# Group norm by chunks of tokens inside the first projection, sample states beside it, and outputs ahead of transposes in the prompt's attention

## The chip, the cores and the metric

The kernel runs on one core of one Trainium2 chip. The time is device microseconds of one execution. TensorE (PE in the rows) multiplies; VectorE (DVE), ScalarE (ACT) and GpSimd (POOL) work on elements; SyncE (SP) issues DMAs. Each engine works through a program of its own, in order, and the programs meet at semaphores.

## The reference, cut to what matters

One inference step of a decoder of two layers, for a prompt of 512 tokens and 8 samples of 4 new tokens: 544 token columns. All is float32; D_MODEL is 1024. Layer 0 mixes a gated convolution with retention in 4 heads:

```python
h, gate_b, gate_c, q, k, v, g = _split(x @ w_in, EVEN_SPLITS)      # 7 x 512 columns
u, conv_hist = causal_dwconv(gate_c * h, conv_hist, conv_w, conv_b)
y_a = gate_b * u
o, ret_state = retention(q, k, v, ret_state, log_gamma)            # chunks of 128 tokens
mu = jnp.mean(o, axis=-1, keepdims=True)                           # over the 128 of a head
var = jnp.mean(jnp.square(o - mu), axis=-1, keepdims=True)
o = ((o - mu) * lax.rsqrt(var + LN_EPS)).reshape(b, t, -1) * gn_g
y_b = jax.nn.silu(g) * o
y = jnp.concatenate([y_a, y_b], axis=-1) @ w_out
```

The samples' matrix state is updated too: 8 samples x 4 heads of 128x128, `state * gamma**4 + k_dec.T @ v`. Layer norms and convolved feed-forward layers follow, and layer 1 has an attention of three branches, whose prompt part is of interest here: softmax over up to 512 keys in a selected and a window branch, then the product with the values.

## The kernel before

Activations lie transposed: features on the 128 partitions, tokens along the row of 544 (`T`), as two halves of 272 (`HT`). A product streams its weights in pieces of 128x1024. ScalarE copies a piece to a rounded high part (`hi`, L1544) and VectorE subtracts to get the low part (`lo`, L1713). TensorE then makes one *stripe* (128 output features): 8 parts of k, each with high x high, high x low and low x high, in two halves, 48 matmuls at L1325, into banks 0 and 1 or 2 and 3 of PSUM. ScalarE takes the even stripes from PSUM into `big` (L1548), VectorE the odd ones (L1720).

The first projection `in0` has 28 stripes: q 0 to 3, k 4 to 7, v 8 to 11, g 12 to 15, c 16 to 19, h 20 to 23, b 24 to 27. After each of the last 16 a *gap* g = 0 to 15 follows, in which TensorE, ScalarE and VectorE run `retention_gap(g)` of their own program. TensorE does the gap's matmuls before the next stripe. The other two do theirs after the `hi` or `lo` of two stripes ahead and after their take, while TensorE is at the next stripe. Gaps 0 to 3 do the rotation, 4 to 11 retention in four chunks of 128 tokens (an even gap: transposes and scores, L1408 to L1418; an odd one: outputs and state, L1430 to L1436), 12 and 13 the same for the samples (13 with 64 small products against the sample states, L1464). Banks 4 to 7 serve these gaps. Gaps 14 and 15 are empty.

GpSimd does the convolution of the four rows c = 0 to 3 (L1993 to L2008). Each waits for stripe 20 + c, multiplies, sums three taps, stores the history, waits for the gate's stripe 24 + c, multiplies by it (L2007, L2008), and only then begins the next row.

After stripe 27 comes the stretch that the change is about, in which no stripe runs. `big[QZ:QZ+4]` are the four heads' outputs over all 544 tokens. Head by head: a mean over partitions as a product with a constant matrix (L1511), subtraction (L1830), square (L1605), a second product (L1519), square root (L1612), reciprocal (L1840), scaling (L1843), the gate (L1847), then the rounded high part on ScalarE (L1599) and the low part on VectorE (L1823). The gate's Silu (L1591) and the convolution's high and low parts (L1594, L1816) come first. Between the heads stand the sample states: VectorE spreads the values (`spread_values`, L1801), TensorE makes two products of 512 columns a head (`state_product`, L1500), VectorE adds them to the states (`new_states`, L1810). TensorE waits for all eight updates, then starts the product `out0`, whose k parts 0 to 3 are the convolution's rows and 4 to 7 the heads. A part can start when its low part is there (`mix_lo`).

In layer 1 the prompt's attention runs 8 rounds of 8 units u (four query tiles, in the order 3,3,0,0,2,2,1,1, each in two branches). A unit is: scores `s` on TensorE (L611), mask and maximum `a` on VectorE (L1036, L1038), exponential `e` on ScalarE (L851), normalization `b` on VectorE (L1046 to L1053), transposes `t` on TensorE (L621), their copy `ta` on ScalarE (L859), outputs `o` on TensorE (L635, L640). TensorE's order in a unit is s(u+2), t(u), o(u-1). VectorE's is b(u), a(u+2); ScalarE's is e(u+1), ta(u). Both t(u) and o(u-1) wait for ta(u-1); t(u) waits for b(u) as well.

## Time and profile before

| | us |
|---|---|
| three runs | 1950.58, 1959.45, 1958.18 |
| median | 1958.18 |
| the profiled execution's own time | 1950.48 |
| its span, first to last instruction | 1948.9 |
| mean granted TensorE clock, share of full | 0.948 |
| stretch from the end of stripe 27 to the first matmul of out0 | 219.52 to 266.06 |

Times of single steps are counted from the start of the span. TensorE is busy for 92% of the span, VectorE for 50%, ScalarE for 35%, GpSimd for 19%. A granted clock of 1.0 is 2.4 GHz and one of 0.5 is 1.2 GHz. The granted clock of a stretch is the mean over it. Matmul ends are modelled, so TensorE's busy time is not all work at its peak.

### The profile page before, as it was taken

What the parts mean: (1) busy time and instruction counts of PE and PEld (TensorE: products, weight loads), DVE (VectorE), ACT (ScalarE), POOL (GpSimd) and SP (SyncE); (2) the same over time, 40 slices, a digit from 0 to 9 for tenths busy, and PEclk for the clock granted to TensorE, in tenths of its full rate; (3) what the DMA queues carried; (4) which work ended last, traced back from release to release, by engine and by line L of the source; (5) the groups of instructions that cost most, each with busy time, mean ns of one, the idle gap of its engine ahead of it and who ended that gap; (6) DMA issues with size and microseconds to landing.
All of it is one profiled execution on the core that took longest, in us unless ns stands there. A gap on an engine that the chain in (4) does not pass through costs nothing.

```text
span 1948.9 us, 34969 instructions
## 1 busy us (share of the span) xinstructions
PE 1793.6 (92%) x13070; PEld 1610.5 (83%) x13070; DVE 980.8 (50%) x1456; ACT 691.2 (35%) x1209; POOL 367.1 (19%) x580
## 2 busy tenths in 40 slices
PE   8999787999999997997888898998979799999996
PEld 8999667999999997996555566665659799999996
DVE  3353287544443435224777755646553644444434
ACT  3222223333332223223666654444432433333222
POOL 0003504000000221001000055544433100000121
PEclk9999679999999998996898999999989899999998
DMA  6221111322222232241000067878652122222331
GB/s 271 87 66 66 39 67 53 101 87 86 86 86 83 89 92 98 87 126 63 1 1 1 1 211 264 286 252 280 197 201 87 58 87 86 86 86 85 90 90 46
DMA packets 89324, 206.17 MB, mean 106 GB/s; under 512 B 13289, under 2 KB 50698, under 8 KB 88466
## 3 DMA queue, kind: packets, MB, share of 16 engines
q1 hardware_dynamic: 71426, 145.00, 23.0%
q0 software_dynamic: 16800, 54.76, 8.3%
q10 hardware_dynamic: 1008, 5.16, 0.6%
q8 instruction: 64, 1.05, 0.2%
q14 instruction: 26, 0.21, 0.0%
HBM read 188.10 MB, written 16.76 MB: 105 GB/s over the span
## 4 chain that ended last, share of the span: by engine, by line
PE 83%; DVE 9%; issue 3%; ACT 3%; DMA 1%; POOL 1%; DVEq 0%; POOLq 0%; ACTq 0%
PE ps L1325 60%; PE ps L691 3%; PE ps L692 3%; PE ps L621 2%; PE ps L635 2%; PE ps L611 2%; PE ps L694 2%; PE ps L803 2%; PE ps L695 2%; DVE slots L1920 1%; DMA slots<-in_slc_v 1%; PE ps L1370 1%; DVE x_parts L1924 1%; DVE big L1912 1%; PE ps L590 1%
## 5 line engine op out<-in xcount | busy, mean ns | idle before, releaser
L1325 PE MATMUL ps<-x_parts,piece_parts 128*128 128x272 f32 x6528 | 839.4, 291 | 41.8 <-DVE x_parts L1924 33.2
L1325 PEld LDWEIGHTS ps<-x_parts,piece_parts 128*128 128x128 f32 x6528 | 831.1, 191 | 48.0 <-issue 26.0
L1713 DVE TENSOR_TENSOR piece_parts<-ring,piece_parts 128x1024 fp32r<-128x1024 f32 (+1 forms) x200 | 244.1, 1221 | 625.4 <-ACT piece_parts L1544 625.4
L1544 ACT ACTIVATE piece_parts<-ring 128x1024 fp32r<-128x1024 f32 (+1 forms) x200 | 208.5, 1043 | 581.5 <-PE ps L1325 562.7
L1325 PE MATMUL ps<-big_parts,piece_parts 128*128 128x272 f32 x2176 | 336.8, 291 | 10.8 <-DVE big_parts L1191 6.4
L1325 PEld LDWEIGHTS ps<-big_parts,piece_parts 128*128 128x128 f32 x2176 | 299.3, 191 | 11.8 <-issue 6.6
L1325 PE MATMUL ps<-hidden_parts,piece_parts 128*128 128x272 f32 x704 | 145.1, 288 | 0.0
L905 ACT ACTIVATE chunk_hi<-slots 128x512 fp32r<-128x512 f32 x128 | 78.8, 628 | 153.6 <-PE ps L694 153.6
L1077 DVE TENSOR_TENSOR slots_low<-slots,chunk_hi 128x512 fp32r<-128x512 f32 x128 | 86.4, 690 | 68.1 <-ACT chunk_hi L905 67.7
L1325 PEld LDWEIGHTS ps<-hidden_parts,piece_parts 128*128 128x128 f32 x704 | 110.6, 189 | 0.0
L2059 POOL COPY slots<-slots 128x2 f32 (+1 forms) x44 | 21.6, 490 | 463.5 <-ACT slots L1673 463.5
L691 PE MATMUL ps<-chunk_hi,x_parts 128*128 128x512 f32 x256 | 104.4, 408 | 3.0 <-ACT chunk_hi L905 2.8
L692 PE MATMUL ps<-chunk_hi,big_parts 128*128 128x512 f32 x256 | 102.6, 401 | 0.0
L621 PEld LDWEIGHTS ps<-rest,slots 128*128 128x128 f32 x320 | 40.8, 161 | 58.2 <-DVE slots L1053 51.6
L621 PE MATMUL ps<-rest,slots 128*128 128x128 f32 x320 | 57.5, 320 | 28.2 <-DVE slots L1053 22.1
L1949 DVE SCALAR_TENSOR_TENSOR slots<-slots,rest 128x560 f32<-128x560 f32 x88 | 70.6, 802 | 12.6 <-DVE slots L1949 4.8
L1681 ACT ACTIVATE slots<-slots 128x512 f32<-128x512 f32 x44 | 27.8, 632 | 135.1 <-DVE slots L1949 135.1
L475 POOL DMA_DIRECT2D slots<-in_cmp_v x128 | 68.9, 539 | 11.7 <-issue 6.8
L851 ACT ACTIVATE slots<-ps,rest 128x512 f32<-128x512 f32 (+3 forms) x128 | 66.1, 525 | 11.0 <-DVE rest L1038 11.0
L691 PEld LDWEIGHTS ps<-chunk_hi,x_parts 128*128 128x128 f32 x256 | 49.3, 192 | 18.8 <-issue 3.8
L2031 POOL TENSOR_TENSOR big<-big,slots 128x544 f32<-128x544 f32 x20 | 35.4, 1769 | 151.8 <-DVE slots L1899 151.8
L859 ACT ACTIVATE slots<-ps 128x1024 f32<-128x1024 f32 (+3 forms) x64 | 45.1, 704 | 50.4 <-PE ps L621 50.4
(312 smaller groups left out, 2004.8 us busy)
## 6 DMA issues: line engine op xcount, KB each, us to landing
ring<-in_w_up SPq DMA_DIRECT2D x88, 512.0 KB, 3.4
ring<-in_w_in SPq DMA_DIRECT2D x48, 512.0 KB, 3.4
ring<-in_w_down SPq DMA_DIRECT2D x32, 512.0 KB, 3.5
slots<-in_cmp_k SPq DMA_DIRECT2D x128, 128.0 KB, 4.6
slots<-in_cmp_v POOLq DMA_DIRECT2D x128, 128.0 KB, 2.7
slots<-in_slc_k SPq DMA_DIRECT2D x128, 128.0 KB, 3.1
slots<-in_slc_v POOLq DMA_DIRECT2D x96, 128.0 KB, 4.4
ring<-in_w_out SPq DMA_DIRECT2D x16, 512.0 KB, 3.5
```

What stands on the lines that cost most here:

```text
L475: eng.dma_start(slots[:, slot, (first + g) * 256:(first + g + 1) * 256], A[cache][bass.ds(v, 1), :, :].rearrange("a p n -> (a p) n")).then ...
L621: mm = pe.transpose(ps[:, 5 + g2, kt * 128:(kt + 1) * 128], prob[:, br, 512 * g2 + kt * 128:512 * g2 + (kt + 1) * 128], K["ident"])
L691: pe.matmul(dst[part], w1_h[:, v, wc[part]], high, start=c == 0, stop=False)
L692: pe.matmul(dst[part], w1_l[:, v, wc[part]], high, start=False, stop=False)
L851: op = act.activation(prob[:, br, 512 * k:512 * k + n], ps[:, 2 * br + k, 0:n], ACT.Exp, bias=nmax[:, br, k:k + 1], accum_out=rsum[:, br, ...
L859: act.activation(pt_b[u % 2][:, 0:8, :].rearrange("p (k t) n -> p k (t n)", k=2)[:, :, 0:n], ps[:, 5:7, 0:n], ACT.Copy).then_inc(UN.sem["t ...
L905: act.activation(chunk_hi[c % 4], rows[:, c, :, :], ACT.Copy).then_inc(chunk_high, 1)
L1077: ve.tensor_tensor(low_rows[:, c, :, :], rows[:, c, :, :], as_f32(chunk_hi[c % 4]), ALU.subtract).then_inc(chunk_low, 1)
L1325: mm = pe.matmul(ps[:, 2 * psum_set + h, 0:HT], split[:, slot % 2, w_part, k * 128:(k + 1) * 128], rhs(k)[v_part][:, h * HT:(h + 1) * HT], ...
L1544: act.activation(split[:, s % 2, 0, 0:size], raw[s][:, 0:size], ACT.Copy).then_inc(w_hi, 1)
L1713: ve.tensor_tensor(split[:, s % 2, 1, 0:size], raw[s][:, 0:size], as_f32(split[:, s % 2, 0, 0:size]), ALU.subtract).then_inc(w_lo, 1)
L1949: ve.scalar_tensor_tensor(out=c, in0=a[:, q:q + CO], scalar=w[:, q:q + 1], in1=c, op0=ALU.mult, op1=ALU.add).then_inc(fd.sem, 1)
```

## The change

The group norm no longer goes by head over all tokens, but by chunk c of tokens over all four heads: chunks 0 to 3 of 128 tokens and a chunk 4 of the 32 sample tokens. Mean, subtraction, square, variance, root and the rest of chunks 0 to 3 move into gaps 6 to 13, each chunk two gaps behind its retention; chunk 4 is done in gaps 14 and 15. The scaling by the reciprocal is one operation over four heads, and the factor `gn_g` and the gate are applied together, in four operations (one a head). The Silu moves to gap 4. The state products move to gaps 14 (three) and 15 (five), with three banks in turn and two buffers for the spread values. Their updates go into the gaps, four of them behind the last low part. On GpSimd the convolved rows stay in place of the c rows, all four convolutions go first, and the four multiplications by the gate follow, each signalled by itself (`conv_y`). High and low parts of convolution and heads are made in gaps 14 and 15 and just behind; `out0` takes its k parts in the order 0, 1, 2, 4, 5, 6, 7, 3. TensorE no longer waits for all eight updates before out0: its last state product waits for the fifth. In the prompt's attention o(u-1) comes before t(u).

```diff
                         elif not end:
                             s(R, u + 2, 1 - gp)
-                        t(R, u)
                         if u:
                             o(R, u - 1, i, gp)
+                        t(R, u)
                     o(R, 7, i, gp)
```

On TensorE:

```diff
+                if c >= 2:
+                    pe.wait_ge(GN["std"], c - 1)
...
+                    pe.wait_ge(GN["cen"], c)
...
+            def head_mean(c):
+                if c < 4:
+                    pe.wait_ge(RA.sem, RA.at("o", c))
+                else:
+                    pe.wait_ge(SA.sem, SA.at("o"))
+                    pe.wait_ge(SV.sem, SV.at("st"))
+                pe.matmul(gn_bank("mean", c), K["mean_h"], big[:, QZ:QZ + 4, GN_TOK[c]], start=True, stop=True).then_inc(GN["mean"], 1)
+
+            def head_var(c):
+                if c < 3:
+                    pe.wait_ge(RA.sem, RA.at("vn", c + 1))
+                elif c == 3:
+                    pe.wait_ge(SA.sem, SA.at("vn"))
+                pe.wait_ge(GN["sq"], c + 1)
+                pe.matmul(gn_bank("var", c), K["mean_h"], gn_buf(gn_sq, c), start=True, stop=True).then_inc(GN["var"], 1)
+
+            def state_product(n):
+                h, u = n // 2, n % 2
+                if n < 3:
+                    pe.wait_ge(GN["std"], 4)
+                else:
+                    pe.wait_ge(st_s, n - 2)
+                if u == 0:
+                    pe.wait_ge(SV.sem, SV.at("vb") + h)
+                pe.matmul(ps[:, (4, 5, 7)[n % 3], :], k_nat[0:32, h * 128:(h + 1) * 128], v_blk[h % 2][0:32, u * 512:(u + 1) * 512],
+                          start=True, stop=True).then_inc(kv_s, 1)
...
+                        if g >= 6:
+                            head_mean((g - 6) // 2)
                         scores_gap((g - 4) // 2)
                     else:
+                        if g >= 7:
+                            head_var((g - 7) // 2)
                         outputs_gap((g - 4) // 2)
                 elif g == 12:
+                    head_mean(3)
                     sample_scores_gap()
                 elif g == 13:
+                    head_var(3)
                     sample_outputs_gap()
+                elif g == 14:
+                    head_mean(4)
+                    for n in range(3):
+                        state_product(n)
+                elif g == 15:
+                    head_var(4)
+                    for n in range(3, 8):
+                        state_product(n)
...
-            pe.wait_ge(SA.sem, SA.at("o"))
-            pe.wait_ge(freed[0], 14)
-            pe.wait_ge(freed[1], 14)
-            for h in range(RH):
...
-            pe.wait_ge(st_s, 8)
```

On ScalarE (the Silu of the whole gate in gap 4, `head_square(c)` in even and `head_std(c)` in odd gaps, not shown):

```diff
+                elif g == 14:
+                    head_square(4)
+                    conv_hi(0)
+                    conv_hi(1)
+                    heads_hi(slice(0, SEQ), 4)
+                elif g == 15:
+                    head_std(4)
...
+            conv_hi(2)
+            heads_hi(slice(SEQ, T), 5)
+            conv_hi(3)
```

On VectorE:

```diff
+            def head_norm(c):
+                o, sd = big[:, QZ:QZ + 4, GN_TOK[c]], gn_buf(gn_sd, c)
+                ve.wait_ge(GN["std"], c + 1)
+                ve.reciprocal(sd, sd).then_inc(GN["rs"], 1)
+                ve.wait_ge(GN["rs"], c + 1)
+                ve.wait_ge(GN["sq"], c + 1)
+                ve.tensor_tensor(o, o, sd, ALU.mult).then_inc(GN["nrm"], 1)
+                ve.wait_ge(GN["nrm"], c + 1)
+                ve.wait_ge(gn_gate, 1)
+                ve.wait_ge(consts_in, 32)
+                for h in range(RH):
+                    op = ve.scalar_tensor_tensor(out=big[:, QZ + h, GN_TOK[c]], in0=big[:, QZ + h, GN_TOK[c]], scalar=K["gn_g"][:, h:h + 1],
+                                                 in1=big[:, GZ + h, GN_TOK[c]], op0=ALU.mult, op1=ALU.mult)
+                op.then_inc(GN["mul"], 1)
...
                     if g % 2 == 0:
+                        if g >= 6:
+                            head_center((g - 6) // 2)
                         scores_gap((g - 4) // 2)
...
+                    if g in (8, 10):
+                        head_norm((g - 8) // 2)
                 elif g == 12:
+                    head_center(3)
                     sample_scores_gap()
+                    head_norm(2)
+                elif g == 13:
+                    ve.wait_ge(SA.sem, SA.at("vn"))
+                    spread_values(0)
+                    head_norm(3)
+                    spread_values(1)
+                elif g == 14:
+                    head_center(4)
+                    new_states(0)
+                    new_states(1)
+                    spread_values(2)
+                    new_states(2)
+                    conv_lo(0)
+                    conv_lo(1)
+                elif g == 15:
+                    heads_lo(slice(0, SEQ), 3)
+                    new_states(3)
+                    spread_values(3)
+                    head_norm(4)
...
+            conv_lo(2)
+            heads_lo(slice(SEQ, T), 5)
+            conv_lo(3)
+            for n in range(4, 8):
+                new_states(n)
```

On GpSimd:

```diff
                 if c:
-                    po.wait_ge(ya.sem, ya.at("ys", c - 1))
+                    po.wait_ge(ya.sem, ya.at("keep", c - 1))
...
+            for c in range(4):
+                po.wait_ge(ya.sem, ya.at("s2", c))
                 po.wait_ge(freed[c % 2], 13 + c // 2)
-                po.tensor_tensor(H_[:, 0:SEQ], conv_c[:, 0:SEQ], B_[:, 0:SEQ], ALU.mult).then_inc(ya.sem, 1)
-                po.tensor_tensor(sample(H_), conv_sample(conv_c), sample(B_), ALU.mult).then_inc(ya.sem, 1)
+                po.tensor_tensor(big[:, HZ + c, :], big[:, CZ + c, :], big[:, BZ + c, :], ALU.mult).then_inc(conv_y, 1)
```

The mean of a chunk goes to bank 7, its variance to bank 5, those of chunk 4 to bank 6; all are single matmuls of 512 (chunk 4: 128) float32 columns.

## Rows read from the trace of the kernel before

**Rows 1.** Page of the profile: busy time of each engine, share of the span, instructions.
```profile
PE 1793.6 (92%) x13070; PEld 1610.5 (83%) x13070; DVE 980.8 (50%) x1456; ACT 691.2 (35%) x1209; POOL 367.1 (19%) x580
```

**Rows 2.** Windows: stretch, its length, busy time by engine, granted clock, DMA share, GB/s.
```profile
219.60:266.05 46.45, 27.42 (x48) 13.07 (x48) 33.32 (x32) 15.30 (x17) 9.90 (x11) 0.58 0.06 18
266.00:281.00 15.00, 14.94 (x98) 14.90 (x99) 8.93 (x9) 1.76 (x3) 0.54 (x1) 0.81 0.44 175
```

**Rows 3.** Timeline of TensorE: start us, length us, what, count, idle before.
```profile
151.78 0.60 PE L1408 MATMUL ps<-rest,big 128*128 128x128 f32 x4
...
153.47 6.26 PE L1325 MATMUL ps<-x_parts,piece_parts 128*128 128x272 f32 x48
...
204.84 14.68 PE L1325 MATMUL ps<-x_parts,piece_parts 128*128 128x272 f32 x96
...
224.10 3.78 PE L1500 MATMUL ps<-slots 32*128 32x512 f32 x4 [0.23 <-DVE slots L1801]
...
258.56 1.98 PE L1500 MATMUL ps<-slots 32*128 32x512 f32 x4 [0.93 <-DVE slots L1801]
...
266.06 14.80 PE L1325 MATMUL ps<-big_parts,piece_parts 128*128 128x272 f32 x96 [4.34 <-DVE slots L1810]
```

**Rows 4.** Groups of instructions by form, 219.6 to 266 us: busy us, mean ns.
```profile
L1840 DVE RECIPROCAL slots<-slots 128x544 f32<-128x544 f32 x4 | 14.2, 3542 | 2.7 <-ACT slots L1612 2.7
...
L1801 DVE TENSOR_TENSOR slots<-slots 32x1024 f32<-32x1024 f32 x4 | 5.2, 1294 | 0.0
L1810 DVE SCALAR_TENSOR_TENSOR slots<-slots,ps 128x512 f32<-128x512 f32 x8 | 5.1, 680 | 0.0
...
L1591 ACT ACTIVATE big<-big 128x2176 f32<-128x2176 f32 x1 | 2.0, 2017 | 0.2 <-DVE big L1720 0.2
...
L1599 ACT ACTIVATE big_parts<-big 128x544 fp32r<-128x544 f32 x3 | 1.9, 645 | 1.7 <-DVE big L1847 1.7
```

**Rows 5.** Timeline of VectorE, single operations between 146 and 233 us.
```profile
146.22 0.87 DVE L1764 SCALAR_TENSOR_TENSOR slots<-slots,ps 128x128 f32<-128x128 f32 x4
153.48 1.23 DVE L1713 TENSOR_TENSOR piece_parts<-ring,piece_parts 128x1024 fp32r<-128x1024 f32 x1 [6.39 <-ACT piece_parts L1544]
...
155.82 0.68 DVE L1754 TENSOR_TENSOR slots<-big,slots 128x512 f32<-128x512 f32 x1
160.92 1.46 DVE L1713 TENSOR_TENSOR piece_parts<-ring,piece_parts 128x1024 fp32r<-128x1024 f32 x1 [4.42 <-ACT piece_parts L1544]
...
188.03 0.39 DVE L1774 TENSOR_TENSOR slots<-big,slots 128x128 f32<-128x128 f32 x1
...
221.85 0.72 DVE L1720 COPY big<-ps 128x544 f32<-128x544 f32 x1
...
230.59 2.42 DVE L1816 TENSOR_TENSOR big_parts<-big,big_parts 128x2176 fp32r<-128x2176 f32 x1 [6.54 <-ACT big_parts L1594]
```

**Rows 6.** Timeline of GpSimd: first and last operation of one convolution.
```profile
154.04 1.82 POOL L1995 TENSOR_TENSOR slots<-big 128x512 f32<-128x512 f32 x1 [121.85 <-ACT big L1548]
...
163.71 0.20 POOL L2005 COPY slots<-slots 128x16 f32<-128x16 f32 x1
```

**Rows 7.** Chain of waits inside one round of the prompt's attention.
```profile
1076.46 1.03 ACT slots L859
...
1077.63 1.94 PE ps L621 x8
1079.57 1.57 PE ps L635 x16
1081.14 0.85 PE ps L611 x4
...
1082.35 1.02 PE ps L635 x16
```

**Rows 8.** Timeline of TensorE: one transpose of the same round, and its wait.
```profile
1087.16 0.88 PE L621 MATMUL ps<-rest,slots 128*128 128x128 f32 x6 [1.21 <-DVE slots L1053]
```

**Rows 9.** Groups of instructions by line, 920 to 1122 us: outputs of the prompt's attention.
```profile
L635 PE MATMUL ps<-slots,ring 128*64 128x128 f32 x640 | 55.2, 309 | 0.8
```

More of the change, by code:

```diff
@@ L235, in build @@
         k_nat, v_nat, s_dec, q_dec, state = (alloc(512, e) for _ in range(5))
-        v_blk = alloc(NB * 128, e)
-        conv_u, conv_c, conv_d = alloc(CW, e), alloc(CO + 2, e), alloc(CO, e)
-        gn_sq, gn_sd = ([alloc(T, e) for _ in range(2)] for _ in range(2))
+        v_blk = [alloc(NB * 128, e) for _ in range(2)]
+        conv_u, conv_c, conv_d = alloc(CW, e), alloc(CO + 2, e), alloc(CO + 2, e)
+        gn_sq, gn_sd = ([alloc(512, e), alloc(512, e), alloc(128, e)] for _ in range(2))
         assert e[0] <= GATES_AT
@@ L338, in build @@
         gn_gate = sem("gn_gate")
-        ya = Steps(sem("conv_pool"), ["hist", "up", "us", "t0", "t1", "s1", "t2", "s2", "keep", "yp", "ys"])
+        ya = Steps(sem("conv_pool"), ["hist", "up", "us", "t0", "t1", "s1", "t2", "s2", "keep"])
+        conv_y = sem("conv_y")
         ret_in = sem("ret_in")
@@ L342, in build, with gn_buf, gn_bank @@
         QZ, KZ, VZ, GZ, CZ, HZ, BZ = 0, 4, 8, 12, 16, 20, 24
-        MIX_H, MIX_L = KZ, [BZ, BZ + 1, BZ + 2, BZ + 3, CZ, CZ + 1, CZ + 2, CZ + 3]
+        MIX_H, MIX_L = KZ, [BZ, BZ + 1, BZ + 2, BZ + 3, GZ, GZ + 1, GZ + 2, GZ + 3]
+        MIX_ORDER = (0, 1, 2, 4, 5, 6, 7, 3)
+        MIX_READY = {0: 1, 1: 2, 2: 4, 3: 6, 4: 5, 5: 5, 6: 5, 7: 5}
+        GN_TOK = [slice(c * 128, c * 128 + 128) for c in range(4)] + [slice(SEQ, T)]
+        def gn_buf(v, c):
+            return v[2 if c == 4 else c % 2].rearrange("p (h n) -> p h n", h=RH)
+        def gn_bank(kind, c):
+            if c == 4:
+                at = 128 * (kind == "var")
+                return ps[:, 6, at:at + 128].rearrange("p (h n) -> p h n", h=RH)
+            return ps[:, 7 if kind == "mean" else 5, :].rearrange("p (h n) -> p h n", h=RH)
         fa = Steps(sem("ffn_act"), ["gelu"])
@@ L1317, in _, with stripe @@
         def _(pe):
-            def stripe(psum_set, slot, ks, rhs, start, stop, ready=None):
-                for k in range(ks):
+            def stripe(psum_set, slot, ks, rhs, start, stop, ready=None, order=None):
+                order = order or range(ks)
+                for k in order:
                     if ready:
@@ L1326, in stripe, with product @@
                                            rhs(k)[v_part][:, h * HT:(h + 1) * HT],
-                                           start=start and k == 0 and w_part + v_part == 0,
-                                           stop=stop and k == ks - 1 and w_part == 1)
+                                           start=start and k == order[0] and w_part + v_part == 0,
+                                           stop=stop and k == order[-1] and w_part == 1)
                 return mm
-            def product(name, rhs, ready=None, gap=None, shift=None):
+            def product(name, rhs, ready=None, gap=None, shift=None, order=None):
                 count = dict((g[0], g[1]) for g in GEMMS)[name]
@@ L1353, in four @@
                             pe.wait_ge(freed[s % 2], SB[name] + i * 2 + s // 2)
-                        stripe(s % 2, s, KC, rhs, True, True, ready if peeled and s == 0 else None).then_inc(pieces, 1)
+                        stripe(s % 2, s, KC, rhs, True, True, ready if peeled and s == 0 else None, order).then_inc(pieces, 1)
                         if gap:
@@ L1489, in retention_gap @@
                     sample_outputs_gap()
-            product("in0", x_parts, lambda k: pe.wait_ge(x0_lo, k + 1), retention_gap)
-            def state_product(h):
-                pe.wait_ge(SV.sem, SV.at("vb") + h)
-                for u in range(2):
-                    n = 2 * h + u
-                    if n >= 2:
-                        pe.wait_ge(st_s, n - 1)
-                    pe.matmul(ps[:, n % 2, :], k_nat[0:32, h * 128:(h + 1) * 128], v_blk[0:32, u * 512:(u + 1) * 512],
-                              start=True, stop=True).then_inc(kv_s, 1)
@@ new lines, in new_states, with head_center @@
+            def new_states(n):
+                h, u = n // 2, n % 2
+                ve.wait_ge(kv_s, n + 1)
+                ve.wait_ge(SP_.sem, SP_.at("o"))
+                st = ret_states[:, 4 * u:4 * u + 4, h, :]
+                ve.scalar_tensor_tensor(out=st, in0=st, scalar=float(gam4[h]),
+                                        in1=ps[:, (4, 5, 7)[n % 3], :].rearrange("p (b e) -> p b e", b=4),
+                                        op0=ALU.mult, op1=ALU.add).then_inc(st_s, 1)
+            def head_center(c):
+                o = big[:, QZ:QZ + 4, GN_TOK[c]]
+                ve.wait_ge(GN["mean"], c + 1)
+                ve.tensor_tensor(o, o, gn_bank("mean", c), ALU.subtract).then_inc(GN["cen"], 1)
@@ L1805, in new_states @@
-            def new_states(h):
-                for u in range(2):
-                    ve.wait_ge(kv_s, 2 * h + u + 1)
-                    ve.wait_ge(SP_.sem, SP_.at("o"))
-                    st = ret_states[:, 4 * u:4 * u + 4, h, :]
-                    ve.scalar_tensor_tensor(out=st, in0=st, scalar=float(gam4[h]),
-                                            in1=ps[:, (2 * h + u) % 2, :].rearrange("p (b e) -> p b e", b=4),
-                                            op0=ALU.mult, op1=ALU.add).then_inc(st_s, 1)
```

142 lines of the change are left out of this document (50 added, 92 removed).

## The prediction

> **What bounds the kernel.** The page comes first: TensorE is busy for 92% of the span, every other engine for half of it or less [rows 1]. So time is to be had where TensorE stands still or runs at half clock. The windows show the place: from 219.60 to 266.05 us, 46.45 us long, TensorE is busy for 27.42 us at a granted clock of 0.58, VectorE for 33.32 [rows 2]. No stripe of weights runs there. The timeline gives the edges: the last two stripes of the first projection end at 204.84 + 14.68 = 219.52, the first stripe of out0 starts at 266.06 [rows 3]. The gap between is 46.5 us. The groups inside it say what fills it: four reciprocals of 3.54 us, the spreading and the state updates on VectorE, one head after the other, each handed to TensorE and ScalarE and back [rows 4]. It began late because GpSimd's last convolution came late. All of this stretch lies on the path to the end, for out0 needs its results.
>
> **What is removed.** The whole stretch of 46.5 us goes. What stays of it must be paid either in TensorE's gaps or behind stripe 27.
>
> **What the gaps cost.** In gaps TensorE's time is the path, since stripes follow each other without a pause: a stripe starts at 153.47 and takes 6.26 us, and gap 8 with its transposes and scores began at 151.78 [rows 3]. A float32 product of 512 columns is two passes: two such products took 1.98 us at full clock and 3.78 us at half clock (4 instructions each), so 0.99 and 1.89 us for one [rows 3]. Four means and four variances of 128 tokens by four heads are 512 columns each, 8 x 0.99 = 7.9 us. Three state products in gap 14 are 3.0 us. The mean of chunk 4 has 128 columns, a quarter, 0.25 us. For ten handoffs I add 0.4 us, an estimate. Sum: 11.6 us. The rows with K = 32 stand for products with K = 128; the columns are the same.
>
> **Whether the others keep up in the gaps.** The worst step is VectorE's at gap 8 (10 is alike). Counted from the end of the stripe: ScalarE's `hi` to 1.2 us; `lo` 1.23; subtracting the mean and three operations of 512 columns at 0.68 [rows 5]; the reciprocal of 512 columns, 3.54 x 512/544 = 3.33 [rows 4]; scaling 0.68; four operations of 128 columns, 0.87 together [rows 5]. That ends at 10.0 us. The next gap opens at 2.8 (the gap, 1.8 before and 1.0 new) + 6.26 = 9.0 us, but needs from this step only what was done by 5.2 us. The `lo` that VectorE then does is needed a stripe later. Its next step is short (1.23 + 0.72 + 0.87, beginning with the next `hi` at 10.2) and ends at 13.0, while gap 10 opens at 9.0 + 3.7 + 6.3 = 19.0: 6.0 us of slack in each pair of steps. Cost: nothing, hidden under stripes; without this cover each such step would cost 4.9 us. ScalarE's Silu (2.02 us [rows 4] and a table load) lies under stripe 17. The steps of ScalarE grow by under 1.5 us of some 8.
>
> GpSimd: one convolution takes 163.91 - 154.04 = 9.9 us [rows 6]. Four in a row, the first from gap 8 on as before, end by about 200 us on the old clock, and the new gaps push stripe 26 later. The rows' gates then come from stripes 24 to 27, so GpSimd waits for them and not they for it. Only the last multiplication follows stripe 27.
>
> Here a rule speaks against the change. First the row: VectorE's `lo` took 1.23 us alone and 1.46 us while GpSimd was in the convolution [rows 5, 6]. In the new kernel both are busy in gaps 8 to 12. By that row two-input operations lose some 0.3 us each, eight of them in a pair of steps 2.4 us, within the 6.0.  The Trainium skill, "SBUF — State Buffer", section "Who interferes with whom", says that a VectorE operation with two SBUF inputs and a GpSimd operation that reads SBUF lock each other out for a whole instruction. By it the loss per operation would be up to a whole GpSimd operation; what that would give is the third rival below, 1945 instead of 1936.5 us.
>
> **The tail behind stripe 27.** Now what is left there, from the end of stripe 27 at 0. VectorE is the chain: `hi` and `lo` until 2.4 and the take of stripe 27, until 3.1; low parts of the heads for 512 tokens, 2048 columns, 2.42 x 2048/2176 = 2.3 [rows 5], to 5.4; one state update 0.68 [rows 4], to 6.0; spreading 1.29 at most [rows 4], to 7.2; norm of chunk 4: reciprocal of 128 columns 0.83 and a handoff, scaling 0.39, four operations of 32 columns, together between 0.3 and 0.87, I take 0.5, to 9.0; then low part of row 2 (0.72), of the heads' 32 tokens (0.39) and of row 3 (0.72), to 10.9; update 4 (0.68), to 11.5. ScalarE's parts (a copy of 544 is 0.65 [rows 4]) run beside it: high part of chunk 4 and of row 3 end at about 10. GpSimd's last row ends near 4.7. TensorE meanwhile does the variance of chunk 4 and products 3 to 5 until 3.4, product 6 when the spreading is done (7.2), and product 7, for which it waits for update 4. That takes 0.99 us, or 1.89 at half clock. I take half clock, since the products at 224.10, 4.6 us behind the last stripe, ran at it with hardly any work between [rows 3]. out0 then starts at 11.5 + 1.9 = 13.4 us; 12.5 at full clock. What was waited for before, all eight updates, is no longer late for anything: three updates run under out0.
>
> out0's start itself: the first two stripes took 14.80 us instead of 2 x 6.26 = 12.5, at a clock of 0.81 [rows 2, 3]. The same wait stands ahead of it, so the same 2.3 us are lost: no gain, no loss. The sample outputs of gap 13, after which stripes 26 and 27 took 14.68 us [rows 3], are as before.
>
> **The attention.** Per round of 24 us I move o(u-1) ahead of t(u), from the rows of one round. Both wait for the same copy. Where t(u) waits for the normalization, as at 1087.16 with 1.21 us [rows 8], the outputs now fill the wait, and the scores behind get away earlier. Where it doesn't, t(u) is later by one output, and so is its copy. At 1077.63 t(1) (1.94) and o(0) (1.57) both run at half clock [rows 7]; in the new order the pair ends at the same 1081.14, but the copy of 1.03 us starts only there, s(4) covers 0.85 of it, and o(1) waits about 0.35 us. This reaches t(4) and is swallowed by its wait, since o(3) has then been done. The round ends within 0.1 us of where it did: 0 for eight rounds. Bounds: if the half clock at this place goes (transposes of 8 in 1.94, those of 6 in 0.88, so 1.1 for 8; outputs 1.57 against 1.02), 1.4 us a round are won, 11 in all. If the 0.35 us stays, 3 are lost; if a second such half-clock piece arises too, 14.
>
> **Sum.** 46.5 - 11.6 - 13.4 = 21.5 us. The profiled execution took 1950.48 us, its span is 1948.9; the change would make 1929.0 of it. That execution is at the low end of the runs, whose median is 1958.18; from the median 21.5 us lead to 1936.7 us, and I predict 1936.5. Its own range is 1929 to 1943, for the tail may be 11 to 18 us, the handoffs 0 to 1.5, and the median of three runs moves by some us (before they span 9).
>
> **Rivals.**
> - *The attention gets faster* (0.12): the outputs fill enough idle time to keep the clock up, 11 us more, 1925.5. For it: the half clock at 1077.63 follows two waits of TensorE. Against: the waits ahead of t(0) and t(1) are of the normalization and the copy, and stay.
> - *The attention gets slower* (0.13): every round keeps the 0.35 us, or a second half-clock piece arises: 3 to 14 us back, 1939.5 to 1950.5.
> - *VectorE and GpSimd hold each other up* (0.10): the slack is gone when each of the eight operations of a pair of steps waits for 0.75 us; at 1.3 us, between half and all of a GpSimd operation of 1.82 [rows 6], VectorE is 10.4 us later, 4.4 past the slack in the pairs at gaps 8 and 10, so 8.8 us are given back: 1945. For it the 1.46 us of `lo`; against, that it is 0.23 more and not 1.3. It is the case that the rule named above speaks of.
> - *No faster, or slower* (0.05): the outputs come onto the chain of t, copy, t in full. They are 55.2 us of TensorE in the stage [rows 9]; all of it exposed gives 1936.5 + 55 = 1992. It decides from 21.5/8 = 2.7 us a round on. Against: the waits ahead of transposes and VectorE's chain, which sets the round, and which needs the scores and not the outputs.
>
> The forecast itself has 0.60.
>
> **Range and chances.** A measurement of this kernel tells about 0.5%, 9.8 us, from no change. The range 1924 to 1948 takes in the faster attention, the lock and most of the slower attention. Faster by over 0.5% are the forecast, the first rival and the lock nearly whole, and most of the second: 0.88. Within 0.5%: 0.09. Slower by more: 0.03.
>
> **What would show it.** The stretch between stripe 27 and out0 lasts 12 to 14 us, with product 7 last in it. Gaps 6 to 12 on TensorE are 1.0 us longer each and stripes 18 to 25 stay at 6.26 us with no waits ahead. GpSimd's four convolutions follow one another from gap 8 on. A round of the attention stays within 0.3 us. The prediction is wrong if TensorE waits in a gap for VectorE's `lo` or for a root, if a table load appears in several gaps (Silu, root and copy alternate there; before, one load each sufficed), or if rounds of the attention change by over 1 us.

## The result, and the profile after

Four runs of the changed kernel took 1931.52, 1929.21, 1927.21 and 1929.44 us, median 1929.33; four of the kernel before have the median 1956.83. The ratio is 0.9864, with a 95% interval from 0.9837 to 0.9891: 26.6 us less (21.3 to 31.9). The forecast was 1936.5, its range 1924 to 1948: the time lies inside, and the gain of 21.5 us was forecast too low. The profiled execution took 1931.52 us, its span is 1929.8 at a mean clock of 0.952.

The page, against [rows 1]: VectorE, ScalarE and GpSimd have nearly the same work as before, TensorE 6.5 us less, in a shorter span.

```profile
PE 1787.1 (93%) x13058; PEld 1604.1 (83%) x13058; DVE 986.4 (51%) x1476; ACT 688.7 (36%) x1212; POOL 372.6 (19%) x580
```

The windows of the tail, of out0's first two stripes and of seven rounds of the prompt's attention (stretch, its length, busy time of TensorE, its weight load, VectorE, ScalarE, GpSimd, the granted clock, DMA share, GB/s). The first two answer to [rows 2]: 46.5 us at 0.58 have become 13.78 at 0.63.

```profile
228.99:242.77 13.78, 7.03 (x12) 2.06 (x12) 11.58 (x17) 3.13 (x6) 4.51 (x3) 0.63 0.18 62
242.70:257.70 15.00, 15.00 (x105) 14.77 (x105) 3.74 (x5) 2.10 (x3) 0.54 (x1) 0.89 0.44 175
924.03:1091.79 167.76, 142.80 (x1168) 90.26 (x1166) 125.17 (x344) 105.84 (x296) 0.00 (x0) 0.92 0.00 1
```

TensorE's timeline (start, length, line, operation, tiles, count, idle before with its releaser) answers to [rows 3]. L1496 is a mean, L1505 a variance, L1516 a state product.

```profile
136.19 1.02 PE L1496 MATMUL ps<-big,slots 128*128 128x512 f32 x2
...
138.73 6.25 PE L1341 MATMUL ps<-x_parts,piece_parts 128*128 128x272 f32 x48
...
211.99 7.79 PE L1341 MATMUL ps<-x_parts,piece_parts 128*128 128x272 f32 x48
219.61 0.38 PE L1496 MATMUL ps<-big,slots 128*128 128x128 f32 x2
...
222.69 6.30 PE L1341 MATMUL ps<-x_parts,piece_parts 128*128 128x272 f32 x48
228.83 0.38 PE L1505 MATMUL ps<-slots 128*128 128x128 f32 x2
229.14 2.84 PE L1516 MATMUL ps<-slots 32*128 32x512 f32 x6
236.65 2.04 PE L1516 MATMUL ps<-slots 32*128 32x512 f32 x2 [4.67 <-DVE slots L1824]
240.77 2.07 PE L1516 MATMUL ps<-slots 32*128 32x512 f32 x2 [2.08 <-DVE slots L1834]
242.77 13.79 PE L1341 MATMUL ps<-big_parts,piece_parts 128*128 128x272 f32 x96
```

Two things are to be seen. In gap 14 the mean of chunk 4 and the first three state products stand between stripes 26 and 27 (219.61 to 222.69) and nothing waits. Behind stripe 27, whose end is 222.69 + 6.30 = 228.99, come two waits, 4.67 us for the spread values and 2.08 us for an update of the states. Then out0 starts, at 242.77.

Where the two profiles part, stage by stage (the edges are matmuls and copies that both traces have; the attention is counted from the first to the eighth copy of its output):

| stage, us | before | after | difference |
|---|---|---|---|
| start to end of stripe 27 | 219.52 | 228.99 | +9.47 |
| tail, to out0 | 46.54 | 13.78 | -32.76 |
| out0 | 63.42 | 62.41 | -1.01 |
| layer 0's rest, to layer 1's first product | 417.03 | 417.31 | +0.28 |
| to the attention's first output copy | 203.69 | 201.54 | -2.15 |
| seven rounds of the attention | 169.47 | 167.76 | -1.71 |
| the samples' attention | 402.60 | 410.85 | +8.25 |
| the rest | 426.63 | 427.16 | +0.53 |

The sum is -19.1 us, 7.5 less than the medians say. The row that stands out is the samples' attention, which the change doesn't touch; without it the sum is -27.3, near the 26.6 of the medians. In the profiles of this study, all with the same code there, it takes 402.6 to 410.9 us, and this pair has both ends of that span. So single profiles can't weigh a few us of the whole; the stages and the repeated runs must do it together.

### The profile page after: what moved, and what is told of

The parts are those of the page before. It is cut to its first block, busy times and chain, and to the rows that moved or that the text cites. A ratio compares the mean times of both kernels' runs of the same rounds, so it can differ in the third digit from the quotient of the medians.

```text
span 1929.8 us, 34978 instructions
## 1 busy us (share of the span) xinstructions
PE 1787.1 (93%) x13058; PEld 1604.1 (83%) x13058; DVE 986.4 (51%) x1476; ACT 688.7 (36%) x1212; POOL 372.6 (19%) x580
## 4 chain that ended last, share of the span: by engine, by line
PE 85%; DVE 7%; ACT 3%; issue 2%; DMA 2%; POOL 0%; SPq 0%; DVEq 0%; POOLq 0%; ACTq 0%
PE ps L1341 61%; PE ps L706 3%; PE ps L707 3%; PE ps L636 2%; PE ps L650 2%; PE ps L818 2%; PE ps L709 2%; PE ps L710 2%; ACT slots L874 1%; PE ps L626 1%; DMA slots<-in_slc_v 1%; DVE slots L1986 1%; PE ps L1386 1%; DVE big L1978 1%; DVE x_parts L1990 1%
## 5 line engine op out<-in xcount | busy, mean ns | idle before, releaser
L650 PEld LDWEIGHTS ps<-slots,ring 128*64 128x64 f32 x640 | 38.2, 149 | 45.5 <-ACT slots L874 39.6
L490 POOL DMA_DIRECT2D slots<-in_cmp_v x128 | 68.9, 539 | 11.8 <-issue 6.9
L650 PE MATMUL ps<-slots,ring 128*64 128x128 f32 x640 | 54.4, 305 | 15.2 <-ACT slots L874 15.2
L636 PE MATMUL ps<-rest,slots 128*128 128x128 f32 x320 | 57.0, 318 | 11.4 <-DVE slots L1068 11.4
```

The lines of the kernel that those rows point to most:

```text
L490: eng.dma_start(slots[:, slot, (first + g) * 256:(first + g + 1) * 256], A[cache][bass.ds(v, 1), :, :].rearrange("a p n -> (a p) n")).then ...
L636: mm = pe.transpose(ps[:, 5 + g2, kt * 128:(kt + 1) * 128], prob[:, br, 512 * g2 + kt * 128:512 * g2 + (kt + 1) * 128], K["ident"])
L650: mm = pe.matmul(out[g2], v_nat_p[:, br, kt, vc[g2]], pt[:, 4 * g2 + kt, :], start=br == 0 and kt == 0, stop=False)
```

## The experiments

The kernels were measured in three sets, each on a chip of its own and together with the kernel before, whose median was 1954.0 to 1954.3 us in all three. Gains in us are that median times (1 - ratio).

### The two halves apart

att_only is the kernel before with the new order of the attention, gn_only the changed kernel with the old order. The diff is that of att_only; gn_only has it the other way round.

```diff
                         elif not end:
                             s(R, u + 2, 1 - gp)
-                        t(R, u)
                         if u:
                             o(R, u - 1, i, gp)
+                        t(R, u)
                     o(R, 7, i, gp)
```

> The kernel before with nothing but the outputs put ahead of the transposes in the prompt's attention. Theory A (the prediction's working: the order is neutral, what differs between the two profiles there is chance): 0 us, within 2 us of before, and the stretch from the start of in1 to the last copy of the attention as long as before, 373.2 us. Theory B (the order itself shortens the rounds, as the two profiles suggest, where this stretch is 369.3 us with the new order): 4 us faster than before, the stretch near 369.

> The changed kernel with the old order in the attention, so the group norm, the states and the convolution alone. Theory A: the whole gain of some 27 us is here. Theory B: 23 to 24 us faster than before, 4 us slower than the changed kernel, and the attention's stretch near 373 us.

att_only: 1949.96 us, ratio 0.9977 [0.9964, 0.9991], a gain of 4.5 us (1.8 to 7.0). gn_only: 1930.53 us, 0.9871 [0.9854, 0.9888], a gain of 25.2 us (21.9 to 28.5). The whole change has 0.9864 in one set and 0.9878 in another (after_again, below): on top of the group norm the new order is worth 0, give or take 3 us, by the ratios. The group norm and the states carry the gain. In gn_only's trace the tail is 13.77 us and out0 62.32, as in the changed kernel.

att_only alone is faster than the kernel before by more than chance, so theory A ("within 2 us") doesn't hold for the repeated runs. Its trace shows it hardly: from layer 1's first product to the eighth copy it takes 372.8 us, the kernel before 373.2. Over all traces without extra matmuls in the attention this stretch takes 373.2 and 375.2 us in the old order (before, gn_only) and 369.1 to 372.8 in the new one (seven traces).

The rounds of the attention vary in both orders: 24.2, 24.2, 23.9, 27.0, 24.1, 23.7 and 22.4 us before, 25.1, 24.2, 22.5, 25.2, 24.0, 22.3 and 24.4 after. TensorE's timeline of the changed kernel shows what varies, t(1) (L636) and o(0) (L650) in two rounds:

```profile
1000.34 1.97 PE L650 MATMUL ps<-slots,ring 128*64 128x128 f32 x16 [0.48 <-ACT slots L874]
1002.24 1.87 PE L636 MATMUL ps<-rest,slots 128*128 128x128 f32 x8
...
1005.23 1.09 PE L650 MATMUL ps<-slots,ring 128*64 128x128 f32 x16 [0.27 <-ACT slots L874]
...
1048.52 1.09 PE L650 MATMUL ps<-slots,ring 128*64 128x128 f32 x16 [0.51 <-ACT slots L874]
1049.55 1.09 PE L636 MATMUL ps<-rest,slots 128*128 128x128 f32 x8
...
1057.01 0.87 PE L636 MATMUL ps<-rest,slots 128*128 128x128 f32 x6 [0.39 <-DVE slots L1068]
```

At 1000.34 the same 16 and 8 matmuls take 1.97 and 1.87 us, at 1048.52 they take 1.09 and 1.09, and the granted clock in the four microseconds around them is 0.50 and 1.00. So the round has a place where the clock falls or doesn't. The old order has a second one: in its round of 27.0 us the six matmuls at 1040.06, behind t(4) and its wait of 1.32 us, take 1.54 us instead of 0.88, and gn_only's round of 26.9 us has the same at 993.05. In the new order the wait ahead of t(4) is 0.39 to 0.50 us, and no round is longer than 25.2. If the clock is the price, then keeping it up must bring both orders to the same shorter round.

### The clock in the attention

Two short matmuls whose result nobody reads are put into each round's first two units, where TensorE waits for VectorE and ScalarE. warm_new has them in the new order, warm_old in the old.

```diff
+            def warm(n):
+                pe.matmul(ps[:, 4, 0:n], K["mean_d"], keep_all[:, 0:n], start=True, stop=True)
...
                             s(R, u + 2, 1 - gp)
+                        if u < 2:
+                            warm(512 - 256 * u)
```

> The changed kernel with two extra matmuls a round of the prompt's attention (512 columns ahead of t(0), 256 columns ahead of o(0); results not used), at the place where TensorE waits and its clock then falls. Theory (the order is neutral at full clock; rounds of 24 to 25 us are such with a half-clock piece in them): rounds of 22.4 us throughout, the seven from the first to the last copy 157 us instead of 168, 8 to 12 us faster than the changed kernel. Rival: the extra matmuls or other waits hold the round up, 24 us a round as before.

> The same two extra matmuls with the old order in the attention (all else as in the changed kernel). If the order is neutral at full clock: rounds of 22.4 us as in warm_new, and both kernels within 2 us of each other. If the new order is itself shorter: 0.3 to 0.5 us a round longer than in warm_new.

warm_new: 1915.02 us, 0.9806 [0.9789, 0.9823]. warm_old: 1918.23 us, 0.9807 [0.9783, 0.9831]. The windows of the seven rounds, first of warm_new, then of warm_old:

```profile
922.10:1079.20 157.10, 142.47 (x1196) 84.67 (x1194) 124.66 (x344) 105.77 (x296) 0.00 (x0) 1.00 0.01 1
```

```profile
928.54:1086.45 157.91, 143.07 (x1196) 85.63 (x1194) 125.92 (x346) 108.24 (x296) 0.00 (x0) 0.99 0.01 1
```

The clock is 1.00 and 0.99 against 0.92, the seven rounds take 157.10 and 157.91 us against 167.76. A round at full clock takes 22.5 us in the new and 22.6 in the old order. That settles two points: at full clock the order is neutral for a round, and what the rounds lose over 22.5 us is the clock. It does not make the two kernels equal: warm_old still has one round of 24.1 us, again with t(5)'s six matmuls at half clock (988.80, 1.54 us), its median is 3.2 us above that of warm_new, more than the 2 us expected, and the two ratios don't tell them apart. The Trainium skill, "TensorE: Matmul & The Clock Gate", section "A second HAM failure mode: psum-queue depth-cycling", says that short idle times of TensorE between groups of matmuls can be frequent enough to make the clock swing, at the cost of throughput. These traces agree: a matmul more in waits of 0.5 to 1.1 us takes the swing away. TensorE's timeline of warm_new at the same place of a round (L661 are the added ones):

```profile
1035.11 1.12 PE L661 MATMUL ps<-rest 128*128 128x512 f32 x2
1036.09 1.09 PE L636 MATMUL ps<-rest,slots 128*128 128x128 f32 x8
...
1038.44 1.09 PE L650 MATMUL ps<-slots,ring 128*64 128x128 f32 x16
```

### Are the outputs on the path?

The matmuls of `o` are done twice, the first time into an unused bank, in the new order (outputs_twice_new) and in the old one (outputs_twice_old).

```diff
                 pt = pt_b[u % 2]
+                for kt in range(qt + 1):
+                    for g2 in range(2):
+                        pe.matmul(ps[half_of[g2], 4, 0:128], v_nat_p[:, br, kt, vc[g2]], pt[:, 4 * g2 + kt, :],
+                                  start=True, stop=True)
```

> The changed kernel with the value products of every unit's outputs issued twice in the prompt's attention (the extra ones into an unused bank, results not used; the compressed part once), 0.4 to 1.2 us of TensorE a unit, some 6 us a round. Outputs on the chain (the slower rival of the prediction): 6 us a round, 48 in all. Outputs mostly hidden in TensorE's waits: under 3 us a round.

> The same with the old order in the attention. If the new order puts more of the outputs on the chain, this loses less than outputs_twice_new; if TensorE's place in the chain is the same in both, as much within 0.5 us a round.

outputs_twice_new: 1944.73 us, 0.9955 [0.9940, 0.9970]; outputs_twice_old: 1947.26 us, 0.9962 [0.9950, 0.9974]. The window of the new one:

```profile
926.28:1109.97 183.69, 161.43 (x1728) 111.16 (x1726) 124.12 (x342) 105.16 (x296) 0.00 (x0) 1.00 0.01 1
```

The clock is at 1.00 here too: busier, TensorE keeps it. In the old order it is 0.98 over the seven rounds (183.40 us); the first two take 27.7 and 27.6 us, the next four, at 1.00, 26.0 to 26.2. The added matmuls of 16, 4, 12 and 8 in a unit take about 0.98, 0.32, 0.75 and 0.54 us from start to start, each twice a round, 5.2 us in all. The rounds at full clock grow from 22.5 to 26.4 us in the new order and from 22.6 to 26.2 in the old: 3.9 and 3.6 us. So some 70% of added output work is on the path in either order. The outputs are not hidden, and at full clock the new order exposes them more by 0.3 us a round at most.

### GpSimd's order

conv_serial lets each convolved row be multiplied by its gate before the next convolution, as before; all else is as in the changed kernel. With the second loop's head gone, its body belongs to the loop over the rows.

```diff
                 po.tensor_copy(sconv_out[:, c, 2:18].rearrange("p (b w) -> p b w", b=NB), us[:, :, 4:6]).then_inc(ya.sem, 1)
-            for c in range(4):
                 po.wait_ge(ya.sem, ya.at("s2", c))
                 po.wait_ge(freed[c % 2], 13 + c // 2)
                 po.tensor_tensor(big[:, HZ + c, :], big[:, CZ + c, :], big[:, BZ + c, :], ALU.mult).then_inc(conv_y, 1)
```

> The changed kernel, in which GpSimd again multiplies each convolved row by its gate before it begins the next row. Theory: rows 1 to 3 then wait for stripes 24 to 26, row 3 is ready about 6 us behind stripe 27, before VectorE gets to its low part at 10.4 us: no difference from the changed kernel, within 1 us. Rival: row 3 is later than 10 us behind stripe 27 and its low part holds out0 up, 1 to 5 us slower.

1930.95 us, 0.9882 [0.9864, 0.9899]; the tail is 14.81 us against 13.78. GpSimd's last multiplication, and two operations of VectorE beside the last convolution:

```profile
236.76 1.32 POOL L2077 TENSOR_TENSOR big<-big 128x544 f32<-128x544 f32 x1
```

```profile
229.69 1.88 DVE L1756 TENSOR_TENSOR piece_parts<-ring,piece_parts 128x1024 fp32r<-128x1024 f32 x1 [1.94 <-ACT piece_parts L1578]
...
237.32 0.92 DVE L1851 TENSOR_TENSOR big<-big,slots 128x128 f32<-128x128 f32 x1
```

The multiplication ends at 238.1, before VectorE wants its row. What costs the microsecond is that VectorE's operations get longer beside GpSimd's: `lo` takes 1.88 us where it takes 1.23 alone, and L1851 takes 0.92 where it takes 0.29 in the changed kernel; the spreading takes 1.50 instead of 1.75. All four convolutions ahead of the multiplications are worth 1.0 us of tail in this pair of traces; the repeated runs (0.9882 against 0.9878 of after_again) don't tell the two kernels apart.

### The tail

VectorE is the chain behind stripe 27. tail_order puts what out0 doesn't need for its start, the low parts of the heads, behind the state updates, and makes update 4 in gap 15's work too. tail_fill leaves the order and keeps TensorE at work in its two waits. tail_both has tail_order and two filler matmuls.

```diff
 # tail_order, VectorE
                 elif g == 15:
-                    heads_lo(slice(0, SEQ), 3)
                     new_states(3)
                     spread_values(3)
+                    new_states(4)
                     head_norm(4)
...
             conv_lo(2)
+            heads_lo(slice(0, SEQ), 3)
             heads_lo(slice(SEQ, T), 5)
             conv_lo(3)
-            for n in range(4, 8):
+            for n in range(5, 8):
 # tail_fill, TensorE (tail_both: only one fill(2), ahead of product 6)
-                    for n in range(3, 8):
+                    for n in range(3, 6):
                         state_product(n)
+                    pe.wait_ge(freed[0], 14)
+                    fill(8)
+                    state_product(6)
+                    fill(2)
+                    state_product(7)
```

`fill` is a matmul of 512 columns into bank 0 whose result nobody reads. In tail_order `out0` waits for conv_lo(2) by its new place.

> The changed kernel, in which VectorE makes state update 3, the last spreading and state update 4 before the norm of chunk 4 and the low parts of the heads, so that TensorE's last two state products need not wait behind those. Theory: the stretch behind stripe 27 is held by VectorE's order alone; out0 starts 6 us earlier (near 7.5 instead of 13.8 us behind stripe 27), and its first stripe doesn't wait for low parts, since its first k parts are ready: 6 us faster than the changed kernel. Rival: the low parts become late, TensorE waits inside the first stripe, and the gain is 1 to 3 us.

> The changed kernel with ten extra matmuls of 512 columns in TensorE's waits behind stripe 27 (eight before state product 6, two before product 7, results not used). Theory: product 7 (2.07 us) and the first stripes of out0 (13.8 us for two) are slow for the clock alone; kept busy, product 7 takes 1.0 and the two stripes 12.5 us, together 2.4 us faster than the changed kernel. Rival: the extra matmuls themselves delay product 6 or the clock falls all the same: 0 to 3 us slower.

> tail_order with two extra matmuls of 512 columns (results not used) ahead of state product 6, where TensorE waited 2.8 us. Theory: products 6 and 7 take 1.1 instead of 1.9 us each and the first two stripes of out0 12.5 instead of 14.4, less up to 1 us of waiting for low parts: 2 to 3.5 us faster than tail_order, out0 from 8 us behind stripe 27. Rival: two are too few, the clock falls all the same, 0 us.

TensorE's timelines behind stripe 27, of tail_order, tail_fill and tail_both in turn:

```profile
234.69 3.75 PE L1517 MATMUL ps<-slots 32*128 32x512 f32 x4 [2.76 <-DVE slots L1825]
238.36 14.37 PE L1342 MATMUL ps<-big_parts,piece_parts 128*128 128x272 f32 x96
```

```profile
231.77 8.83 PE L1522 MATMUL ps<-slots 128*128 128x512 f32 x16
240.53 1.12 PE L1516 MATMUL ps<-slots 32*128 32x512 f32 x2
...
244.55 12.31 PE L1341 MATMUL ps<-big_parts,piece_parts 128*128 128x272 f32 x96
```

```profile
231.56 3.21 PE L1523 MATMUL ps<-slots 128*128 128x512 f32 x4
234.70 2.41 PE L1517 MATMUL ps<-slots 32*128 32x512 f32 x4
237.04 2.51 PE L1342 MATMUL ps<-big_parts,piece_parts 128*128 128x272 f32 x18
239.90 10.03 PE L1342 MATMUL ps<-big_parts,piece_parts 128*128 128x272 f32 x78 [0.35 <-DVE big_parts L1878]
```

tail_order: 1925.15 us, 0.9848 [0.9831, 0.9865]; out0 starts 9.4 us behind stripe 27 instead of 13.8, but products 6 and 7 run at half clock and out0's start in part, so that products 6 and 7 take 3.75 us and out0's first two stripes 14.37. tail_fill: 1930.92 us, 0.9881 [0.9861, 0.9902], no gain: its eight fillers last until 240.5, 4 us longer than the spreading, which ended at 236.5 in the changed kernel, and what the clock gives back (products at 1.12 instead of 2.07, two stripes in 12.31 instead of 13.79) just pays for it. tail_both: 1921.26 us, 0.9841 [0.9822, 0.9860]: the two fillers last until 234.7, while VectorE's spreading ended at 234.24, so they outlast the wait by less than half a microsecond; the four product matmuls take 2.41 us, out0 starts at 8.4. In the traces the tail is 1.0 and out0 1.5 us shorter than in tail_order, as expected (2 to 3.5); the intervals of the two ratios overlap nearly whole, so the repeated runs don't show it.

### All together, and the changed kernel again

all_three is the changed kernel with tail_both and warm. after_again is the changed kernel unchanged, in the same set.

> The changed kernel with VectorE's tail order of tail_order, the two extra matmuls of tail_both and those of warm_new. If the parts add: 6 us from the tail and 12 to 14 from the attention, some 1909 us, 45 us faster than the kernel before. Rival: what the attention gives depends on where its start falls, and the sum is 4 us or more short of that.

> The changed kernel as it is, once more, to set the order's share against gn_only (25.2 us faster than before): 25 us if the order in the attention gives nothing on top of the group norm, 28 to 30 if its 4 us of att_only add.

all_three: 1909.74 us, 0.9789 [0.9775, 0.9804]. after_again: 1928.88 us, 0.9878 [0.9863, 0.9894], a gain of 23.8 us. all_three is 19.1 us faster than the changed kernel and, by the ratio, 41.2 (38.3 to 44.0) faster than the one before, the fastest of this study. By the medians the parts add up as expected (1909); by the ratios 45 was to be had, and the sum is 4 us short, with intervals that overlap. In the trace of all_three the tail is 7.6 us and the seven rounds are 157.1.

## Why the prediction was right, point by point

**The stretch removed, gaps and tail paid.** The mechanism was right, the sum 2.8 us too low. Forecast: 46.5 - 11.6 - 13.4 = 21.5. Traces: 46.54 - 9.47 - 13.78 + 1.01 = 24.3, and by repeated runs of gn_only 25.2. The terms:

- *Means and variances.* 0.99 us each was read from the length of a pair of products; from start to start one takes less. In gap 6 the step from the mean to the stripe is 138.73 - 136.19 = 2.54 us where before it was 1.68: 0.86 each, 6.9 instead of 7.9 for eight.
- *Gap 14.* 222.69 - 219.61 = 3.1 us, where 3.25 was forecast.
- *Handoffs.* 0.4 was forecast, none was paid: no matmul in gaps 6 to 13 waits.
- *The place around gap 13.* "As before" was wrong by 1.2 us in favour: the two stripes, 14.68 in [rows 3], now take 7.79 + 6.30 = 14.09, and the sample outputs ahead of them are 0.6 us shorter as well.
- *Start.* At the stripe behind gap 5 (129.22 before, 130.09 after), ahead of the first added matmul, the changed kernel's trace was already 0.9 us later. The added part of the 9.47 us is so 8.6; 6.9 + 3.1 - 1.2 make 8.8 of it, and 0.2 has no place.
- *Out0's first stripes.* 13.79 us instead of the 14.80 of [rows 3] that I held as unchanged: 1.0 in favour.

**The tail.** Here the chain of waits of the changed kernel shows each link that the prediction named:

```profile
231.32 0.72 DVE big L1763
232.03 2.20 DVE big_parts L1868
234.23 0.60 DVE slots L1834
234.83 1.67 DVE slots L1824
236.50 0.87 DVE slots L1848
...
237.73 0.75 DVE big L1856 x4
...
238.81 0.56 ACT big_parts L1616
...
240.03 0.69 DVE slots L1834
...
240.77 2.07 PE ps L1516 x2
```

The take of stripe 27, the low parts of 512 tokens (2.20 of 2.3), one update, the spreading, the norm of chunk 4, then update 4 and product 7 at half clock. Product 6 starts at 7.7 us behind stripe 27 (forecast 7.2), product 7 at 11.8 (11.5), with 2.07 us (1.89), out0 at 13.78 (13.4). The one term off was the spreading, 1.75 us where 1.29 was called "at most"; with no operation of GpSimd beside it it takes 1.21 (at 208.62). GpSimd stands beside it here: in VectorE's and GpSimd's timelines the two meet.

```profile
231.95 2.28 DVE L1868 TENSOR_TENSOR big_parts<-big,big_parts 128x2048 fp32r<-128x2048 f32 x1
...
234.75 1.75 DVE L1824 TENSOR_TENSOR slots<-slots 32x1024 f32<-32x1024 f32 x1
```

```profile
232.18 3.25 POOL L2078 TENSOR_TENSOR big<-big 128x544 f32<-128x544 f32 x1 [8.78 <-DVE big L1763]
```

GpSimd's multiplication of 544 columns takes 3.25 us beside VectorE's low parts (231.95, two inputs) and 1.32 alone (conv_serial, above); it ends at 235.43, inside the spreading. In conv_serial that multiplication comes later, but a sum of GpSimd (until 235.35) reaches into the spreading, which lasts 1.50 us.

**Whether the others keep up.** They did, though two terms were too small. The groups of gaps 4 to 13 give the reciprocal 3.34 us (forecast 3.33), the scaling 0.87 (0.68), the gate's four operations 4 x 0.42 = 1.7 (0.87). The last was twice the forecast, for it was read from operations with an operand in PSUM and beside no GpSimd: the four take 1.14 us at 207.57, where GpSimd rests, and 1.98 and 1.49 at 164.01 and 183.20, where it works. With the third operation of 512 columns (L1797), which also grew, the steps at gaps 8 and 10 are 1.5 and 2.0 us longer than forecast, from a slack of 6.0.

```profile
L1848 DVE RECIPROCAL slots<-slots 128x512 f32<-128x512 f32 x4 | 13.3, 3337 | 0.0
...
L1856 DVE SCALAR_TENSOR_TENSOR big<-big,rest 128x128 f32<-128x128 f32 x16 | 5.7, 420 | 0.1
```

ScalarE's tables are no cost either: it loads one for the Silu at 122.46 and one for the root at 146.15, and no more in these gaps.

**VectorE and GpSimd hold each other up** (0.10). The contention is there, 1.9 us for one multiplication, 1.1 for one operation of VectorE in gap 10, but it did not reach TensorE in a gap: that needed 0.75 us for each of eight operations on the pair's chain, and the whole step was at most 2.0 us longer, of a slack of 6.0. In the tail it costs at most the 0.5 us of the spreading.

```profile
176.87 1.80 DVE L1797 TENSOR_TENSOR slots<-big,slots 128x512 f32<-128x512 f32 x1
```

```profile
176.84 1.29 POOL L2061 TENSOR_TENSOR slots<-big 128x512 f32<-128x512 f32 x1
```

VectorE's operation takes 0.68 us alone and lost 1.12 here, where GpSimd's, begun 0.03 us earlier, had 1.26 to go. So it is in most such pairs: the one that starts second loses nearly what the first has left. The multiplication in the tail lost 1.93 us of 2.05, the `lo` of 1.88 in conv_serial 0.65 of 0.80, L1851 there 0.63 of 0.76. The Trainium skill, "SBUF — State Buffer", section "Who interferes with whom", calls the ports that VectorE and GpSimd share an exclusive lock, and these four fit that. Two do not: the `lo` of 1.46 in [rows 5] lost 0.23 us where GpSimd's multiplication by a scalar had 1.34 left, and the `lo` at 173.93 of the changed kernel, beside the same kind of operation, lost none. So the rival's mechanism is real, and its size was wrong: an operation of VectorE pays only for what is left of the one it meets, and few meet one.

**The attention.** "The round ends within 0.1 us of where it did" is right for a round at full clock, 22.5 against 22.6 us, and the local steps are in the rows above: o(1) waits 0.27 us for its copy (0.35 forecast), and the wait ahead of t(4) fell from the 1.21 of [rows 8] to 0.39. What was wrong is the bound on a real round, 0.3 us, and "rounds change by over 1 us", named as a sign that the prediction is wrong, did appear. Rounds moved by up to 2.0 us either way in the pair shown and by 4.4 in after_again (27.0 to 22.6), because the half-clock pieces came at other places. That this nearly cancels over eight rounds was not worked out; in this the 0 of the sum was luck. Over seven rounds it came to -1.7 in one pair of profiles, +0.4 from before to after_again (169.47 to 169.89), and -4.5 us for att_only in repeated runs. Neither "the attention gets faster" (11 us) nor "slower" (3 to 14) happened. The argument moved the matmuls of one round by hand and left out that in the old order a half-clock piece can stand behind the wait ahead of t(4) too; no trace of the new order has one there. Wrong too was a reason given against the last rival, that VectorE's chain sets the round and not the outputs: at full clock some 70% of added output time is on the path. The rival fell all the same, since this is so in both orders.

**What stays open.** Whether the new order is worth anything in the whole kernel. Alone it gained 4.5 us, on top of the group norm nothing that can be measured; the intervals (1.8 to 7.0, and 0 give or take 3) overlap, so one gain of 1.8 to 3 us would fit both. The traces lean that way: 373.2 and 375.2 us in the old order against 369.1 to 372.8 in the new, and at least one piece behind t(4) at half clock in each of the three old-order traces whose outputs are not doubled, none in the new order. No run was made to settle it. Why the samples' attention takes 402.6 to 410.9 us with the same code: in the pair shown, its clock is 0.96 before and 0.94 after, but what decides between them was not tried.

## What to carry to other kernels

A stretch in which engines hand small work to each other can be moved between stripes by another way of cutting it (by tokens instead of by heads), at the price of its matmuls alone, as long as each step of the other engines fits under a stripe; cost matmuls from start to start and not by their length, and sum the last engine's work behind the last stripe in order. Reordering matmuls that wait for the same copy was neutral at full clock here, so look at the granted clock first: a short matmul in a wait that comes in every round can be worth more than the order. A filler must not outlast the wait by more than the clock gives back: eight outlasted it by 4 us and gained nothing.

## What the runs showed of the hardware

- Two small matmuls a round (1.6 us of TensorE from start to start) made rounds of mostly 24 to 25 us into 22.5 and gave, from set to set, 14 us in the new order (1929.3 to 1915.0) and 12 in the old (1930.5 to 1918.2).
- The clock can be low where TensorE never rests. In the windows of the changed kernel from 204.79 to 228.99 us it is busy for all of 24.20 us, in part with small products of 4 columns, at a clock of 0.79:

```profile
204.79:228.99 24.20, 24.20 (x141) 22.26 (x140) 10.58 (x15) 5.06 (x7) 1.82 (x1) 0.79 0.07 23
```

- Doubling the outputs kept the clock at 1.00 in the new order (0.98 in the old) without any filler, so part of the added work paid for itself: eight rounds with 5.2 us more are 42, and the medians rose by 15.9 us in the new order (1928.9 to 1944.7) and 16.7 in the old (1930.5 to 1947.3).
